# Three chunks of the next expert wait in a second place, GpSimd copies them home, and a block's products change order and kind

## The reference

```
def moe(x, w_router, b_router, w_up, b_up, w_down, b_down):
    logits = (xt @ w_router + b_router).astype(jnp.float32)
    top_v, top_i = lax.top_k(logits, TOP_K)
    top_w = jax.nn.softmax(top_v, axis=-1)
    gates = jnp.sum(jax.nn.one_hot(top_i, N_EXPERTS) * top_w[..., None], axis=1)
    for e in range(N_EXPERTS):
        hid = xt @ w_up[e] + b_up[e]
        x_glu = jnp.minimum(hid[:, :D_EXPERT], SWIGLU_LIMIT)
        x_lin = jnp.clip(hid[:, D_EXPERT:], -SWIGLU_LIMIT, SWIGLU_LIMIT)
        act = x_glu * jax.nn.sigmoid(SWIGLU_ALPHA * x_glu) * (x_lin + 1)
        y = act @ w_down[e] + b_down[e]
        out = out + gates[:, e:e + 1] * y
```

## Time and profile before

| what | value |
|---|---|
| median of 3 runs | 1288.15 us |
| the profiled execution | 1288.93 us, span 1287.2 us, granted clock 0.985 |
| busy | TensorE 1207.2 us (94%), VectorE 372.5 us (29%), ScalarE 185.8 us (14%), GpSimd 59.2 us (5%) |
| DMA | 454.40 MB, mean 353 GB/s; 429 GB/s in most slices of the expert stage |
| chain that ended last | TensorE 52%, DMA 39%, VectorE 4% |
| blocks of experts | 35 |

### The profile page before, as it was taken

The page is one execution under the profiler, slowest core; times in us unless marked ns, Lnnn a source line. Parts: engine busy times, 40 slices in busy tenths (PEclk is TensorE's granted clock), DMA queues, the critical chain, the costliest instruction groups (busy, mean ns, idle before and its releaser), DMA issues.

```text
span 1287.2 us, 15187 instructions
## 1 busy us (share of the span) xinstructions
PE 1207.2 (94%) x5850; PEld 536.9 (42%) x5851; DVE 372.5 (29%) x737; ACT 185.8 (14%) x360; POOL 59.2 (5%) x89
## 2 busy tenths in 40 slices
PE   5899999889999999999999999999999999999996
PEld 1888655453343433333333333333443333333342
DVE  1944364631321112222111111122211122211114
ACT  2200264110111001110010000011110011101001
POOL 2230053000000000000000000000000000000000
PEclk9899999979999999999999999999999999999998
DMA  9973488309499999999999999999699999999590
GB/s 372 369 208 131 160 258 318 130 27 383 184 415 429 430 428 429 427 429 430 428 429 427 429 430 428 429 428 403 256 416 429 429 427 429 428 428 429 238 391 33
DMA packets 49044, 454.40 MB, mean 353 GB/s; under 512 B 16736, under 2 KB 16776, under 8 KB 20320
## 3 DMA queue, kind: packets, MB, share of 16 engines
q1 hardware_dynamic: 48064, 450.90, 84.7%
q0 software_dynamic: 512, 1.72, 0.4%
q10 hardware_dynamic: 448, 1.50, 0.4%
HBM read 453.06 MB, written 1.05 MB: 353 GB/s over the span
## 4 chain that ended last, share of the span: by engine, by line
PE 52%; DMA 39%; DVE 4%; issue 2%; ACT 1%; SPq 0%; POOL 0%; DVEq 0%; POOLq 0%
DMA ring<-in_moe_w_up 37%; PE pair L1201 23%; PE pair L1248 9%; PE pair L1010 9%; PE pair L1091 2%; DMA ring<-in_ada_w 2%; PE pair L1187 1%; PE pair L1026 1%; PE pair L968 1%; DVE hT_mem L899 1%; PE pair L1036 1%; PE pair L1049 1%; DVE v_mem L905 1%; DVE v_mem L906 1%; PE pair L1135 1%
## 5 line engine op out<-in xcount | busy, mean ns | idle before, releaser
L1201 PE MATMUL pair<-ring,v_mem 128*64 128x512 f32 x2240 | 495.8, 594 | 29.6 <-DMA ring<-in_moe_w_up 29.2
L1201 PEld LDWEIGHTS pair<-ring,v_mem 128*64 128x64 f32 x2240 | 181.1, 137 | 336.0 <-issue 274.5
L1248 PE MATMUL pair<-ring,v_mem 128*64 128x512 f32 x1120 | 248.1, 595 | 1.5
L905 DVE TENSOR_SCALAR v_mem<-pair 128x512 f32<-128x512 f32 x35 | 24.2, 692 | 719.8 <-PE pair L1211 719.8
L1248 PEld LDWEIGHTS pair<-ring,v_mem 128*64 128x64 f32 x1120 | 92.5, 137 | 132.9 <-issue 132.7
L579 ACT ACTIVATE v_mem<-v_mem 128x512 f32<-128x512 f32 x35 | 22.1, 630 | 538.8 <-DVE v_mem L905 538.8
L899 DVE TENSOR_TENSOR hT_mem<-hT_mem,pair 128x512 f32<-128x512 f32 x140 | 89.4, 680 | 8.0 <-PE pair L1187 8.0
L1187 PE MATMUL pair<-v_mem 64*128 64x512 f32 x280 | 78.8, 641 | 3.4 <-ACT v_mem L591 0.8
L1127 PE MATMUL pair<-q_mem,pT_mem 128*64 128x512 f32 x288 | 71.5, 618 | 1.3 <-DVE pT_mem L848 1.3
L379 POOL TENSOR_TENSOR rstd<-ms,neghalf 128x1 f32<-128x1 f32 (+1 forms) x8 | 4.7, 594 | 1071.7 <-DVE ms L627 1071.7
L591 ACT ACTIVATE v_mem<-pair 128x512 f32<-128x512 f32 x35 | 20.9, 597 | 228.7 <-PE pair L1248 228.7
(11 more groups left out here) (217 smaller groups left out, 944.5 us busy)
## 6 DMA issues: line engine op xcount, KB each, us to landing
ring<-in_moe_w_up SPq DMA_DIRECT2D x128, 2048.0 KB, 23.2
ring<-in_moe_w_down SPq DMA_DIRECT2D x64, 2048.0 KB, 20.3
ring<-in_ada_w SPq DMA_DIRECT2D x24, 1024.0 KB, 8.4
ring<-in_na_w_qkv SPq DMA_DIRECT2D x12, 1024.0 KB, 27.4
ring<-in_na_w_o SPq DMA_DIRECT2D x4, 1024.0 KB, 15.1
tokens<-in_na_rpb SPq DMA_DIRECT2D x32, 96.0 KB, 6.4
gain<-in_norm_g POOLq DMA_DIRECT2D x3, 512.0 KB, 5.7
tokens<-in_x SPq DMA_DIRECT2D x1, 1024.0 KB, 5.0
```

The lines of the kernel that those rows point to most:

```text
L905: d.tensor_scalar(glu, bank[0][:, :], LIMIT, None, ALU.min).then_inc(glu_ready, 1)
L1201: last = mm(bank[half][64 * n:64 * n + 64, :], xT[:, k % 4, 64 * (k // 4):64 * (k // 4) + 64], w[:, c0:c0 + HALF], start=k == 0, stop=False)
L1248: last = mm(bank[2][64 * n:64 * n + 64, :], aT[:, j, 64 * half:64 * half + 64], w[:, HALF * n:HALF * n + HALF], start=k == 0, stop=k == KC ...
```

## The change

It has three parts.

**Staging.** The three attention buffers become one tensor `zone` of 6 MB. Once the attention is done with a third of it, chunk 0, 1 or 2 of expert 1 is loaded into it. From then on SP loads chunks 3, 4 and 5 of an expert into the ring as before, and then chunks 0 to 2 of the expert after it into `zone`, each as soon as the chunk that lay there has been copied. GpSimd copies every such chunk (128 x 4096 float32) to its place in the ring when TensorE has freed that place, and gives `staged[j]`; TensorE waits for `staged[j]` instead of `expert_in[j]` for chunks 0 to 2. A one-element addition goes ahead of each copy (`home_free[j]`).

**Order in a block.** The last two slices of the up product are split by half: both slices of the gated half, its bias, `glu_done`; then those of the linear half, its bias, `up_done`. VectorE clips `glu` at `glu_done`, multiplies it by the sigmoid, and then makes `lin` and `act`; the sum of part 0 comes after `act`.

**Sums.** `comb` holds ones instead of gates. Two small products (line 1299) bring each slot's gate into PSUM; ScalarE copies it (`gate_slot`), scales `y` by it on its way out of PSUM and rounds the result to float32r (`y_high`); VectorE adds the rest (`y_low`). `combine` is then four float32r products instead of two float32 ones.

The small tensors move: `xT`, `glu`, `lin`, `sig` into `hT_mem`, `aT`, `y` and `combT` into the `mod` buffers, the residual into `row_mem`, the biases into `gain` and `mod[0]`. The loads of the residual and of the biases go later on ScalarE's queue.

```diff
+PER, UPS, STAGED = 6, 4, 3
+        zone = sb("zone", [P, ZONE, 2048])
...
         def expert_chunk_here(eng, e, j):
-            eng.wait_ge(expert_in[j], e * 16 + 16)
+            if j < STAGED:
+                eng.wait_ge(staged[j], e + 1)
+            else:
+                eng.wait_ge(expert_in[j], e * 16 + 16)
...
+            def second_half(e):
+                blocks_before = sp.value_load(ends_i[0:1, bass.ds(e - 1, 1)], ...)
+                for j in range(STAGED, PER):
+                    sp.wait_ge(ring_free, blocks_before * PER + (EXP - PER + j + 1))
+                    load_expert(e, j, expert_chunk(j))
+            with sp.Fori(1, E - 1) as e:
+                second_half(e)
+                for j in range(STAGED):
+                    sp.wait_ge(staged[j], e + 1)
+                    load_expert(e + 1, j, staged_chunk(j))
...
+            with pool.Fori(1, E) as e:
+                for j in range(STAGED):
+                    pool.wait_ge(expert_in[j], e * 16 + 16)
+                    pool.wait_ge(staged[j], e)
+                    pool.wait_ge(home_free[j], e)
+                    pool.wait_ge(ring_free, blocks_before * PER + (EXP - PER + j + 1))
+                    g.tensor_tensor(home_mark[:, j:j + 1], mark, mark, ALU.add).then_inc(home_free[j], 1)
+                    g.tensor_copy(expert_chunk(j), staged_chunk(j)).then_inc(staged[j], 1)
...
+                s.activation(gate_slot, bank[4][:, TOK:TOK + 1], ACT.Copy).then_inc(slot_gates, 1)
-                s.activation(y, bank[2][:, :], ACT.Copy).then_inc(y_ready, 1)
+                s.activation(y_high, bank[2][:, :], ACT.Copy, scale=gate_slot).then_inc(y_ready, 1)
...
+                ve.wait_ge(glu_done, b + 1)
+                d.tensor_scalar(glu, bank[0][:, :], LIMIT, None, ALU.min).then_inc(glu_ready, 1)
+                ve.wait_ge(sig_ready, b + 1)
+                d.tensor_tensor(glu, glu, sig, ALU.mult).then_inc(pre_ready, 1)
                 ve.wait_ge(up_done, b + 1)
                 d.tensor_scalar(lin, bank[1][:, :], LIMIT, -LIMIT, ALU.min, ALU.max).then_inc(lin_ready, 1)
-                d.scalar_tensor_tensor(act, lin, 1.0, glu, ALU.add, ALU.mult).then_inc(pre_ready, 1)
+                d.scalar_tensor_tensor(act, lin, 1.0, glu, ALU.add, ALU.mult).then_inc(act_ready, 1)
                 add_part(0, b, is_first)
-                d.tensor_tensor(act, act, sig, ALU.mult).then_inc(act_ready, 1)
...
+                d.scalar_tensor_tensor(y_low, bank[2][:, :], gate_slot, y_high, ALU.mult, ALU.subtract).then_inc(y_split, 1)
...
                 for n in range(2):
-                    mm(bank[banks[n]][:, :], combT[...], y[...], start=True, stop=True)
+                    mm(bank[banks[n]][:, :], combT[...], y_high[...], start=True, stop=False)
+                for n in range(2):
+                    mm(bank[banks[n]][:, :], combT[...], y_low[...], start=False, stop=True)
```

More of the change, by code:

```diff
@@ L83, in build @@
         h2 = q_mem[:, :].rearrange("p (t d) -> p t d", t=2)
[L84 to L96, removed]
+        v = v_mem.rearrange("p (t d) -> p t d", t=4)
+        tmp = acc
+        last_tmp = v_mem[:, 0:2048].rearrange("p (t d) -> p t d", t=2)
+        last_junk = v_mem[:, 2048:3072]
         mod_high, mod = [], []
@@ L776, in _ @@
                 d.scalar_tensor_tensor(scale2[:, h], bank[i][:, :], 1.0, gain[:, h], ALU.add, ALU.mult).then_inc(bc_dve, 1)
+            ve.wait_ge(in_gain, 48)
+            for i in range(2):
+                ve.wait_ge(bc_done, 6 + i + 1)
+                h = slice(HALF * i, HALF * i + HALF)
+                d.tensor_tensor(gate2[:, h], bank[2 + i][:, :], gain[:, h], ALU.mult).then_inc(bc_dve, 1)
+            ve.wait_ge(bc_dve, 6)
             ve.wait_ge(in_bup, 16)
@@ L1206, in block_step @@
                         make_tables()
+                expert_chunk_here(pe, e, UPS - 1)
                 pe.wait_ge(bsel_ready, b + 1)
-                for half in range(2):
-                    for n in range(2):
-                        c0 = D * half + HALF * n
-                        last = mm(bank[half][64 * n:64 * n + 64, :], bsel, bup_parts[:, c0:c0 + HALF],
-                                  start=False, stop=True)
-                last.then_inc(up_done, 1)
+                up(0, KC - 2)
+                up(0, KC - 1)
+                add_bias(0).then_inc(glu_done, 1)
+                up(1, KC - 2)
+                up(1, KC - 1).then_inc(ring_free, 1)
+                add_bias(1).then_inc(up_done, 1)
                 if is_first:
@@ L1222, in block_step @@
                 for t in range(2):
-                    last = tr(bank[4][:, P * t:P * t + P], comb[:, t, :, :].rearrange("p a s -> p (a s)"), ident[:, :])
+                    tr(bank[4][:, P * t:P * t + P], comb[:, t, :, :].rearrange("p a s -> p (a s)"), ident[:, :])
+                for t in range(2):
+                    last = mm(bank[4][:, TOK:TOK + 1], comb[:, t, :, :].rearrange("p a s -> p (a s)"), gate_tok[:, t:t + 1],
+                              start=t == 0, stop=t == 1)
                 last.then_inc(combT_done, 1)
```

159 lines of the change are left out of this document (100 added, 59 removed).

## The result

The changed kernel takes 1384.24 us (median of 4 runs, 1376.94 to 1391.63), the kernel before 1287.64: 1.0749 of its time, 95% interval 1.069 to 1.0809. It is slower, as forecast, but by 96.6 us where about 49 were forecast. The four runs of the changed kernel lie 15 us apart, and the two longer ones show the lower mean granted clock (0.932 and 0.933, against 0.940 and 0.943). The profiled execution took 1382.31 us with a span of 1380.6, against 1287.2 before.

A forecast was written before the change was run, and what follows sets the result against it. TensorE bounds first and after DMA holes, otherwise weight loads at 29.36 us per expert. Blocks +44.3, block 0 +5.5, tail -0.4: +49.4 on 1288.9 gives 1338 us; range 1290 to 1385, likeliest case 1320 to 1360.

The forecast's parts named there:

- The holes: DMA engines' idle times near double experts, 15.0 us; claimed as large in sum as before, so staging gains 0 there.
- The copy's length: GpSimd's copy of a 128x4096 chunk, claimed to take 3.7 us, with ends at 2.5 and 5.5 us.
- its start in the block: GpSimd starts copying 14.7 us after the block's up products start, 0.4 us ahead of `act`.
- the count: Blocks whose `act` meets a copy: 27 at 30.2 us; 3 second blocks at 28.6, 4 undisturbed at 27.1.
- holes-close rival: DMA holes at double experts close, the last two each giving back up to 14.7 - 2.5 us: 1265 us, chance 0.06.
- The copying block: Expert block where a copy holds `act` and delays `combine(1)`: 30.0 us, taken as 30.2 with the bias selector.
- the bias selector: Copy within SBUF behind the sum, may meet the second copy: up to 0.9 us per block, 0.2 taken.
- the clock: Rival: TensorE standing some 2.5 us per block lowers its clock, some 4 us more per block: 1440 us, chance 0.03.
- The prelude: Before block 0: moving residual, biases and gate row costs nothing while loads land in time, else up to 2 us.
- Block 0: First block's `glu` and `act` run into three copies started at 287 us: +5.5 us (0 to 8).
- the second blocks of double experts: Copies every 4.0 us, the third ending at 15.4, delay the first product by 1.5 us: 28.6 us blocks.
- The rest of a block: Undisturbed block: sums -0.86, gate products +0.45, gate copy +0.25 on 27.3, so 27.1 us.

The follow-up runs named there:

- experiment 3: Changed kernel with each GpSimd copy cut to one column of 4096, loads and waits kept (output wrong): 1289.49 us, 1.0019 of the kernel before.
- experiment 2: Changed kernel with one operand of each of VectorE's two products in PSUM, staging and copies kept: 1294.81 us, 1.0067 of the kernel before.
- experiment 1: Changed kernel without staging: SP loads all six chunks into the ring, new order and sums kept: 1284.48 us, 0.9978 of the kernel before.
- experiment 7: Changed kernel with eight more matmuls per block into a free bank ahead of `combine(1)`: 1368.70 us, 1.0628 of the kernel before.
- Experiment 6: Kernel of experiment 2, with SP also waiting for the gain row before the first staged load: 1288.72 us, 1.0014 of the kernel before.
- experiment 4: Changed kernel with each copy cut into eight pieces of 512 columns, back to back: 1453.73 us, 1.1288 of the kernel before.
- experiment 5: Changed kernel with each copy in four pieces, a semaphore wait and one-element addition between pieces: 1297.47 us, 1.0083 of the kernel before.
- experiment 10: Kernel of experiment 9 with VectorE's order from before the change, one-pass sums kept: 1271.61 us, 0.9884 of the kernel before.
- experiment 9: Changed kernel without copies, nine chunk places in rotation, TensorE's code for 30 middle experts written in a row: 1263.44 us, 0.982 of the kernel before.

## Why the prediction was right, and where its sizes were off

- *Direction and mechanism:* right. The holes stay (experiment 3), the copies hold VectorE's product and TensorE waits behind it (experiment 2), and taking staging away leaves a small gain (experiment 1). The copy's length (3.59 for 3.7) and its start in the block (14.66 for 14.7) were right to 0.1 us, and so was the count: each of the 27 blocks meets a copy again. Experiment 2 speaks against the holes-close rival as well.
- *The copying block, 30.2 forecast, 31.72 measured.* This term was mis-sized, 27 times 1.52, 41 of the 44 us that were missing. It has two parts. The smaller, 0.3: the bias selector meets the second copy in each block and delays the copy of the transposed `act` (L973) behind it, so a block at full clock takes 30.5 (I had given it 0.2 of up to 0.9). The larger, 1.2 on average: the clock. I had made the clock a rival of its own, 4 us in every block or nothing, with a chance of 0.03. It came on top of the forecast case, with some 1.4 us in 8 of the 27 blocks and 2.5 in 8 others, and experiment 7 shows it by giving most of it back. The error was to treat as a separate case what is a consequence of the forecast wait. The row for it stood there, from a wait of 4.66 us; here 2.5 were enough in 16 of 27 blocks.
- *The prelude, 0 forecast (up to 2), 5.2 measured.* I asked whether the moved loads land in time, and not what the staged loads of 2 MB each do to a 4 KB row that is issued among them: a load of 2 MB alone takes 7.6 us to land, and behind such loads the row lands 13.53 us after its issue, with VectorE waiting for it. TensorE works on through the output projection meanwhile and waits behind VectorE afterwards. Experiment 6 shows the cause.
- *Block 0, 5.5 forecast, 7.9 measured.* Copies that follow one another don't let the product in between: it takes 6.63 us, held through the rest of one copy and all of the next. Experiments 4 and 5 show the same with smaller pieces, and what ends it. For the second blocks of double experts I was 1.4 us too high: copies follow every 3.69 us and not 4.0, so the third ends at 14.6 and the product (1.43 us) loses 0.74.
- *The rest of a block, -0.16 forecast (27.1), -0.55 measured.* The sum was near, but its parts were wrong. With VectorE's old order the one-pass sums give nothing (experiment 10: 27.28 against 27.30). There TensorE's load of weights for `combine(1)` waits 1.0 us for VectorE's addition before the change and in experiment 10 alike, so what the first sum saves is waited, and behind the second one TensorE waits 0.45 us for ScalarE's copy of `combT`, which now stands behind the gate copy. The order, which I had priced only as the time at which products meet copies, gives 0.53, because `act` comes ahead of the addition and the transposes find it ready.
- *Sum:* 41.0 + 5.2 + 2.4 - 4.2 - 1.0 = 43.4 of the 44.0 us between the forecast +49.4 and the measured +93.4; the last block and the tail, where I had forecast a gain of 0.6, make up the rest. The forecast's own range of 1320 to 1360 missed it. That the wide one, 1290 to 1385, held the median by 1 us is luck: it left the clock out, and two of the four runs (1386.17 and 1391.63 us) lie above it.

## What to carry to other kernels

A wait that a change adds to a lagging engine can have a second price, as here where TensorE stood for some 2.5 us: add the lower clock to the forecast itself, not as a case beside it. Give small rows that are needed soon their turn ahead of large early loads. Before copying on GpSimd, read which of VectorE's instructions have all operands in SBUF; one operand in PSUM, or gaps in the copies, took away nearly the whole loss. More places for weights help only if the load order uses them: three spare places with a fixed home gained nothing here, even with nearly free copies (experiment 3), while the same three in rotation took 21 us off the kernel without staging (experiments 1 and 9), 1.6%.

## What the runs showed of the hardware

- A GpSimd copy of 128x4096 float32 takes 3.588 us (93 of them, 3587 to 3591 ns); 1024 columns take 1.03, 512 columns 0.61.
- A lone copy held VectorE's `act` until its end. The Trainium skill ("SBUF — State Buffer", "Who interferes with whom") says that a VectorE instruction with two SBUF inputs contends with a GpSimd instruction that reads SBUF, and that casts and tensor_scalars can contend too when they run in their 2-port modes. The trace agrees with the first. It shows a cast and tensor_scalars held (the 96x64 cast takes 3.28 us where it takes 0.18 alone), but not in which mode they ran. What I had not expected is that eight GpSimd instructions back to back were one hold of 4.4 us, and that a semaphore wait between pieces ended it.
- With a wait of 2.5 us in each copying block, the down products took longer, at the lower level of TensorE's clock, in 16 of 27 blocks, mostly in a turn of three. With a wait of 3.4 us (experiment 4) it was 27 of 27, with fillers in the wait (experiment 7) four of 27. Why the turn is as it is stays open.
- Each of four jumps back over TensorE's code of six blocks left it standing 3.7 to 4.3 us, at the lower clock behind it. The code of 30 blocks in a row did not stop, nor does the changed kernel, whose loop jumps back over the code of one block each time. The Trainium skill ("Runtime: NRT & Kernel Launch", "Instruction fetch mechanics") says that a taken branch stalls when its target lies outside the window of fetched pages; the two runs agree.
